# Latents tile by tile from split operands, and other buffers and orders in one hybrid encoder layer

## What is computed

```
h = rmsnorm(x, g_mix);  proj = h @ w_in          # 1024 tokens x 1024
(gq, gk, gv, gr, gaf, gab, cq, ckv, kr, gates) = split(proj)
y_a = gated linear attention of gq, gk, gv, gaf, gab (4 heads, both directions), rmsnorm, silu(gr), @ w_gla_out
q = rmsnorm(cq) @ w_uq;  kv = rmsnorm(ckv) @ w_ukv   # 8 heads, 128 + 64 rotary, values 128
y_b = softmax attention of q, k (rmsnorm per head, rope), v, @ w_mla_out
x = x + (sigmoid(gates_a) * y_a + sigmoid(gates_b) * y_b) @ w_o
h = rmsnorm(x, g_ffn);  16 experts, each takes its top 128 tokens by router softmax
x = x + sum over experts of value * (silu(h @ w_gate) * (h @ w_up)) @ w_down
```

## Time and profile before

| | us |
|---|---|
| runs | 2054.45 median of 3, 2053.08 to 2058.4 |
| profiled execution | 2054.51 |
| its span | 2052.8 |
| TensorE busy | 1939.7 (94%) |
| VectorE busy | 1268.2 (62%) |
| ScalarE busy | 981.9 (48%) |
| mean granted clock of TensorE | 0.981 |
| DMA | 303.11 MB, mean 148 GB/s; 364 GB/s from 1560 on |

### The profile page before, as it was taken

The page is one execution under the profiler, slowest core; times in us unless marked ns, Lnnn a source line. Parts: engine busy times, 40 slices in busy tenths (PEclk is TensorE's granted clock), DMA queues, the critical chain, the costliest instruction groups (busy, mean ns, idle before and its releaser), DMA issues.

```text
span 2052.8 us, 25988 instructions
## 1 busy us (share of the span) xinstructions
PE 1939.7 (94%) x9268; PEld 1605.5 (78%) x9268; DVE 1268.2 (62%) x1660; ACT 981.9 (48%) x1588; POOL 119.4 (6%) x127
## 2 busy tenths in 40 slices
PE   7989999999999999999899999999289999999997
PEld 5677888888778787878688888887278888888886
DVE  4157777777865646565311222432978989898986
ACT  4155555555454334242311211322268787878785
POOL 2010000000000000000000000000001010101010
PEclk9999999999999999999999999999699999999999
DMA  6000000000311111120412311152789999999992
GB/s 238 0 17 12 21 18 22 22 22 6 107 53 43 53 42 52 31 62 9 156 52 65 110 52 52 62 208 90 282 312 380 400 394 399 395 398 397 397 398 80
DMA packets 138658, 303.11 MB, mean 148 GB/s; under 512 B 16208, under 2 KB 70864, under 8 KB 138576
## 3 DMA queue, kind: packets, MB, share of 16 engines
q1 hardware_dynamic: 133968, 285.20, 37.3%
q0 software_dynamic: 4608, 16.78, 3.2%
HBM read 272.58 MB, written 29.36 MB: 147 GB/s over the span
## 4 chain that ended last, share of the span: by engine, by line
PE 87%; DVE 8%; ACT 2%; issue 1%; DMA 1%; POOL 1%; SPq 0%; DVEq 0%; ACTq 0%; POOLq 0%
PE ps L827 21%; PE ps L829 21%; PE ps L828 21%; PE ps L780 6%; PE ps L851 5%; PE ps L808 2%; PE ps L809 2%; PE ps L1042 1%; PE ps L885 1%; PE ps L884 1%; PE ps L1054 1%; DVE row_max L1445 1%; PE ps L1148 1%; PE ps L1026 1%; DVE top_i L1780 1%
## 5 line engine op out<-in xcount | busy, mean ns | idle before, releaser
L1264 DVE TENSOR_TENSOR w_lo<-w_raw,w_hi 128x1024 fp32r<-128x1024 f32 x384 | 442.7, 1218 | 57.8 <-ACT w_hi L2180 57.6
L2180 ACT ACTIVATE w_hi<-w_raw 128x1024 fp32r<-128x1024 f32 x384 | 370.9, 1052 | 12.6 <-PE ps L829 8.0
L1264 DVE TENSOR_TENSOR d_lo<-d_raw,d_hi 128x1024 fp32r<-128x1024 f32 x58 | 71.0, 1224 | 311.9 <-ACT d_hi L1972 311.8
L1972 ACT ACTIVATE d_hi<-d_raw 128x1024 fp32r<-128x1024 f32 x58 | 61.5, 1061 | 308.9 <-PE ps L829 296.9
L827 PE MATMUL ps<-w_hi,xeT_hi 128*128 128x512 f32 x512 | 201.8, 394 | 7.1 <-DVE xeT_lo L1264 7.1
L829 PE MATMUL ps<-w_hi,xeT_lo 128*128 128x512 f32 x512 | 200.1, 391 | 0.0
L828 PE MATMUL ps<-w_lo,xeT_hi 128*128 128x512 f32 x512 | 200.0, 391 | 0.0
L827 PE MATMUL ps<-hT_parts,d_hi 128*128 128x512 f32 x384 | 152.2, 396 | 8.5 <-ACT sg L2105 7.7
L828 PE MATMUL ps<-hT_parts,d_hi 128*128 128x512 f32 x384 | 150.6, 392 | 0.0
L829 PE MATMUL ps<-hT_parts,d_lo 128*128 128x512 f32 x384 | 150.6, 392 | 0.0
L1445 DVE TENSOR_REDUCE row_max<-ps 128x1 f32<-128x1024 f32 x64 | 78.3, 1224 | 106.6 <-PE ps L885 105.9
(11 more groups left out here) (313 smaller groups left out, 4006.7 us busy)
## 6 DMA issues: line engine op xcount, KB each, us to landing
w_raw<-in_w_gate_e SPq DMA_DIRECT2D x128, 512.0 KB, 8.0
w_raw<-in_w_up_e SPq DMA_DIRECT2D x128, 512.0 KB, 7.5
w_raw<-in_w_down_e SPq DMA_DIRECT2D x128, 512.0 KB, 6.7
d_raw<-in_w_in SPq DMA_DIRECT2D x80, 256.0 KB, 3.0
xs<-in_x SPq DMA_DIRECT2D x8, 512.0 KB, 6.9
rows_T<-hT SPq DMA_DIRECT2D x1, 4096.0 KB, 12.8
mla_out_T<-obS SPq DMA_DIRECT2D x16, 256.0 KB, 2.0
carry<-rows_T SPq DMA_DIRECT2D x1, 4096.0 KB, 14.2
```

What stands on the lines that cost most here:

```text
L1264: return dve.tensor_tensor(dst, whole, high.bitcast(F32), ALU.subtract)
L1972: nc.scalar.activation(d_hi[:, n % 2, :], d_raw[:, n % 2, :], ACT.Copy).then_inc(d_hi_ok, 1)
L2180: nc.scalar.activation(w_hi[:, n % RING, :], w_raw[:, n % RAW, :], ACT.Copy).then_inc(hi_ok, 1)
```

## The change

Start and latents. `w_lat` is loaded raw, in four pieces behind x tile 0, and split with the gain inside: ACT `w_lat_hi`, DVE `w_lat_lo`. x is no longer transposed in 16 groups first; `latents(t)` multiplies tile t with `three`, and after its k = 2 transposes tile t + 1 (`x_rows_T`), which ACT splits (`x_high`), DVE completes (`x_low`) and ACT copies to `hT` without the gain (`x_whole`); the gain goes into `rows_high` and `rows_low` at the last head. The transposes of the first half of the latents stand inside tiles 5 to 7 (`LAT_STEP`), with two PSUM banks in turn; those of the second half stand between the first four and the last four projection groups of head 0, which now run 4, 5, 0, 1, 6, 7, 2, 3. `lat_r` lies in `xs`. `hT` is stored in halves, and `load_a2(0)` is issued ahead of it.

GLA heads. The second direction has its own `zT_back`; `gate_bias(1)` does not wait for `ed_ok` and stands ahead of the tail subtraction.

Merge. `sg` lies at 16.5 S, beside `oT_hi` and `oT_lo`; ACT's wait for `oa_out` moves to `branch_hi`.

Experts. In DVE's list of the first turn `rows_in(1)` stands at u = 0 and 2 and `activate(0)` at u = 3; in ACT's list the second part of `rows_in(1)` at u = 6, not 8.

The semaphores `head_ms`, `o_ms`, `x1_ms` and their partners become `mean_sq` and `rstd`, counted through.

```diff
+FIRST_ORDER = (4, 5, 0, 1, 6, 7, 2, 3)
+LAT_STEP = {(5, 4): (0,), (5, 6): (1,), (6, 4): (2,), (6, 6): (3,), (7, 1): (4,), (7, 3): (5,), (7, 5): (6,)}
 @@ memory
-                        w_lat = sb_in(lat_mem, "w_lat", [P, KD, LAT])
-                        lat_r = sb_in(lat_mem, "lat_r", [P, NT, LAT])
+                        lat_r = xs[:, :, 0:LAT]
+                        xT_hi = sb_in(lat_mem, "xT_hi", [P, 2, KD, P], F32R)
+                        xT_lo = sb_in(lat_mem, "xT_lo", [P, 2, KD, P], F32R)
+                    zT_back = sb_in(gla_tmp, "zT_back", [P, S])
-                    sg = sb_in(merge_mem, "sg", [P, 2, S])
+                        sb_in(sg_mem, "below_sg", [P, 16 * S + HALF])
+                        sg = sb_in(sg_mem, "sg", [P, 2, S])
 @@ SyncE
+            load_x(0)
+            sp.dma_start(g_mix_c[:], col(g_mix, KD), allow_slow_non_contiguous=True).then_inc(g_mix_in, 16)
+            for j in range(4):
+                sp.dma_start(w_lat_raw[:, 2 * j:2 * j + 2, :],
+                             w_in_k[:, 2 * j:2 * j + 2, C_LAT:C_LAT + LAT]).then_inc(wlat_in[j], 16)
+            for t in range(1, NT):
+                load_x(t)
 @@ TensorE
+            def x_rows_T(t):
+                pe.wait_ge(xn, t + 1)
+                for b in range(2):
+                    if t:
+                        pe.wait_ge(hT_ok, 2 * t - 1 + b)
+                        pe.wait_ge(xT_lo_ok, 2 * t - 1 + b)
+                    transpose4(b, P, [xs[:, t, (4 * b + j) * P:(4 * b + j + 1) * P] for j in range(4)]).then_inc(hT_tr, 1)
+            def latents_T(c):
+
                 half, j = divmod(c, 7)
                 pe.wait_ge(lat_n, 4 * half + 4)
+                if 2 <= c < 7 or c >= 11:
+                    back = 2 if c < 7 else 4
+                    pe.wait_ge(latT_dve if c % 2 == 0 else latT_act, (c - back) // 2 + 1)
...
+            def latents(t):
+                if t >= 2:
+                    pe.wait_ge(lat_ev, t - 1)
+                a = 4 + 2 * ((t + 1) % 2)
+                hi, lo = xT_hi[:, t % 2], xT_lo[:, t % 2]
+                for k in range(KD):
+                    if k % 4 == 0:
+                        pe.wait_ge(xT_lo_ok, 2 * t + k // 4 + 1)
+                    if t == 0:
+                        pe.wait_ge(wlat_lo_ok, k + 1)
+                    first, last = k == 0, k == KD - 1
+                    three(ps[:, a, 0:LA], hi[:, k, :], lo[:, k, :], w_lat_hi[:, k, 0:LA], w_lat_lo[:, k, 0:LA],
+                          first, last)
+                    mm = three(ps[:, a + 1, 0:LB], hi[:, k, :], lo[:, k, :], w_lat_hi[:, k, LA:LAT],
+                               w_lat_lo[:, k, LA:LAT], first, last)
...
+                    if k == 2 and t + 1 < NT:
+                        x_rows_T(t + 1)
+                    for c in LAT_STEP.get((t, k), ()):
+                        latents_T(c)
...
-            for g in range(4, 8):
+            for g in FIRST_ORDER[0:4]:
                 project(0, g)
-            for g in range(4):
+            for c in range(7, 14):
+                latents_T(c)
+            pe.wait_ge(latT_dve, 7)
+            pe.wait_ge(latT_act, 7)
+            for g in FIRST_ORDER[4:8]:
                 project(0, g)
 @@ VectorE
+            x_mean(0)
             dve.wait_ge(g_mix_in, 16)
+            x_scale(0)
+            for k in range(2):
+                w_lat_low(k)
+            x_low(0, 0)
+            x_low(0, 1)
+            for k in range(2, KD):
+                w_lat_low(k)
+            x_mean(1)
+            x_scale(1)
             dve.wait_ge(small_in, 16 * small_loads)
...
             for t in range(NT):
+                if t + 1 < NT:
+                    x_low(t + 1, 0)
+                    x_low(t + 1, 1)
                 if t:
                     lat_scale(t - 1)
+                if t + 2 < NT:
+                    x_mean(t + 2)
+                    x_scale(t + 2)
+                for c in {6: (0,), 7: (2, 4)}.get(t, ()):
+                    latents_T_in(c)
+                if t == NT - 1:
+                    latents_T_in(6)
+                lat_in(t)
+                lat_mean(t)
...
             def k_mean(h):
-                dve.wait_ge(head_sq, 16 * h + 8)
+                dve.wait_ge(head_sq, 2 * group_count(h, 7))
...
                 def gate_bias(d):
                     dve.wait_ge(z_mm, h * 2 + d + 1)
-                    if d == 1:
-                        dve.wait_ge(ed_ok, h * 2 + 1)
...
                     if d == 1:
                         dense_lo(4, mine)
+                    else:
+                        gate_bias(1)
...
                     if d == 0:
-                        gate_bias(1)
                         dense_lo(3, mine)
...
-                    if first and u in (4, 8):
-                        rows_in(1, (u // 4 - 1,))
+                    if first and u in (0, 2):
+                        rows_in(1, (u // 2,))
+                    if first and u == 3:
+                        activate(0)
 @@ ScalarE
+            act.wait_ge(consts, 4)
+            act.wait_ge(small_in, 16 * small_loads)
+            for t in range(NT):
+                if t + 1 < NT:
+                    for b in range(2):
+                        x_high(t + 1, b)
+                    for b in range(2):
+                        x_whole(t + 1, b)
+                if t + 2 < NT:
+                    x_square(t + 2)
...
+                for c in {6: (1,), 7: (3, 5)}.get(t, ()):
+                    latents_T_in(c)
+                lat_squares(t)
...
-            act.wait_ge(oa_out, 16 * GH)
...
+                        act.wait_ge(oa_out, 16 * GH)
                         act.wait_ge(oa_back, 16 if k < 6 else 32)
```

More of the change, by code:

```diff
@@ L80, with mean_count @@
 EARLY_ROWS = 2
+HEAD_MEANS = 2 * NT
+GLA_MEANS = HEAD_MEANS + 2 * MH
+FFN_MEANS = GLA_MEANS + 2 * GH
+def mean_count(what, t):
+    if what == 0:
+        return t + 1 if t < 2 else 2 * t - 1
+    return 2 * t + 4 if t < NT - 2 else NT + t + 1
 def seam_at(i, n):
@@ L357, in hybrid_layer @@
         small_in = sem("small_in")
-        wlat_in = sem("wlat_in")
+        wlat_in = [sem(f"wlat_in{j}") for j in range(4)]
+        wlat_hi_ok = sem("wlat_hi_ok")
+        wlat_lo_ok = sem("wlat_lo_ok")
         g_mix_in = sem("g_mix_in")
@@ new lines, in w_lat_low, with x_low @@
+            def w_lat_low(k):
+                dve.wait_ge(wlat_hi_ok, k + 1)
+                dve.scalar_tensor_tensor(out=w_lat_lo[:, k, :], in0=w_lat_raw[:, k, :], scalar=g_mix_c[:, k:k + 1],
+                                         in1=w_lat_hi[:, k, :].bitcast(F32), op0=ALU.mult,
+                                         op1=ALU.subtract).then_inc(wlat_lo_ok, 1)
+            def x_low(t, b):
+                dve.wait_ge(xT_hi_ok, 2 * t + b + 1)
+                rows = slice(4 * b, 4 * b + 4)
+                low_part(xT_lo[:, t % 2, rows, :], ps[:, b, :].rearrange("p (a c) -> p a c", a=4),
+                         xT_hi[:, t % 2, rows, :]).then_inc(xT_lo_ok, 1)
@@ L1349, in _ @@
-            for c in range(0, 14, 2):
-                dve.wait_ge(lat_tr, c + 1)
-                dst, src, gain = lat_out(c)
-                dve.tensor_scalar(dst, src, gain, None, ALU.mult).then_inc(latT_dve, 1)
+                if t + 2 < NT:
[6 more added lines that the diff above has]
+                lat_in(t)
@@ L1354, in rotate @@
+                lat_mean(t)
+            lat_scale(NT - 1)
+            for c in range(8, 14, 2):
+                latents_T_in(c)
             def rotate(dst, src, tmp, steps, parts=(0, 1)):
@@ L1977, in out_hi @@
                 nc.scalar.activation(wo_hi[:, u - 2, :], d_raw[:, u % 2, :], ACT.Copy).then_inc(d_hi_ok, 1)
-            for g in range(4, 8):
+            for g in FIRST_ORDER[0:4]:
+                take(0, g)
+            for c in range(7, 14, 2):
+                latents_T_in(c)
+            for g in FIRST_ORDER[4:6]:
                 take(0, g)
             v_high(0)
-            for g in range(4):
+            for g in FIRST_ORDER[6:8]:
                 take(0, g)
+            act.wait_ge(h_out, 32)
+            act.wait_ge(lat_tr, 14)
             for c in (4, 5, 6, 7):
@@ L2207, in turn @@
                 for u in range(UNITS):
-                    if first and u in (4, 8):
-                        rows_in(1, (u // 4 - 1,))
+                    if first and u in (4, 6):
+                        rows_in(1, (u // 2 - 2,))
                     split(FIRST + u, e)
```

274 lines of the change are left out of this document (141 added, 133 removed).

## The result

The changed kernel takes **2026.21 us** (median of 4 runs, 2024.85 to 2030.54), the kernel before 2054.33 in the same series (2053.08 to 2058.40). The ratio is **0.9863, 95% interval 0.9843 to 0.9883**. The forecast was 2028.7 in a range of 2015 to 2044. The profiled execution has a span of 2024.5 us for 2052.8, 28.3 less.

A forecast was written before the change was run, and what follows sets the result against it. TensorE, busy 94% of the span, was taken as the bound: its work plus waits. Start -6.9, GLA heads -8.5, merge -3.3 and experts -7.1 sum to -25.8, from 2054.5 to 2028.7 us; range 2015 to 2044.

The forecast's parts named there:

- Start: Latents to first scores: first scores at 136.7 us against 143.6, so -6.9, bounds -11 to +10.
- this cover: Start: small loads landing at 24.2, then DVE's angles of 6.2 us, hold tile 1's latents until 31.1.
- The k step: Latents: six narrow products, 2208 columns, take 1.00 us; far bound 1.36.
- Rival 1: Latents: narrow products no quicker than 512-column ones, step 1.36, total 2045.5 us; chance 0.08.
- the waits 0.93 and 3.13: Tiles 6 and 7: TensorE waits 0.9 and 3.3 us for DVE's copies ahead of `latents_T(2)` and `latents_T(4)`.
- rivals 3 and 4: Start: 3, waits in every tile keep the clock low, 2076, chance 0.05; 4, gain lost in waits, 2047 to 2059, 0.07.
- the slow stretch behind the wait at tile 7: Latents: 1.6 us added for TensorE running slow after its 3.3 us wait at tile 7.
- GLA: GLA heads: four waits for `zT`, 6.9 us, go, with a slow stretch of 1.6: -8.5, bounds -5 and -9.5.
- Merge: Merge's start: ACT, freed from `oaS`'s store, waits for a weight landing at 984.2: -3.3, bounds -1 and -8.
- Experts: First expert's turn: `rows_in(1)` ahead of `activate(0)` and first splits moves TensorE's transposes earlier: -7.1, bounds -5 and -8.
- The other edits: Gain in `rows_high` and `rows_low`, shared semaphores, earlier `load_a2(0)`, halved h store: worth nothing, under 1 us without cover.
- Rival 2: Waits of the start or merge absent, or a stretch at full clock: 10 to 14 us more, 2015 to 2018; chance 0.10.

The follow-up runs named there:

- the eight: Eight profiles whose start is the changed kernel's code: its own two and six kernels with later parts undone or altered; first scores 136.5 to 142.1 us, median 139.3.
- Experiments 1 and 2: Changed kernel with one shared `zT` in the old order: 2039.5 us; with `zT_back` kept but `gate_bias(1)` back behind `decay`: 2034.2 us (one run).
- second profile: The changed kernel, nothing altered, profiled and run once more: 2030.9 us, first scores at 140.8 us.
- the median of nine: Nine profiles that have the changed kernel's code at the merge's start; that part runs from 42.3 to 43.8 us, median 43.2.
- Experiment 4: Changed kernel with the merge's third weight unit issued ahead of the 3 MB read of `mT`, not behind it: 2021.3 us, ratio 0.9831.
- 9 to 11: Changed kernel with angles behind tile 0: 2023.7 us; DVE's copies first: 2024.0; start reordered: 2016.9, and with the merge's unit ahead of the read: 2010.4.
- the last two kernels: Changed kernel with the start reordered: 2016.9 us; the same with the merge's third weight unit ahead of the 3 MB read: 2010.4 us.

## Why the prediction held, point by point

**Start, -6.9 forecast; -7.1 in the first profile, some -4 over the eight.** Step by step: small loads issued last at 20.85 and landed at 24.7 (24.2 forecast), angles 6.2 us, tile 1 at 31.55 (31.1). DVE's timeline, which answers to the earlier trace rows, shows this cover exactly:

```profile
24.71 0.15 DVE L1390 TENSOR_SCALAR qhn_c<-qhn_c 128x1 f32<-128x1 f32 x1 [5.35 <-DMA w_router_s<-in_w_router]
...
30.60 0.29 DVE L1414 TENSOR_SCALAR cos_t<-cos_t 128x256 f32<-128x256 f32 x1
30.81 1.28 DVE L1314 TENSOR_TENSOR xT_lo<-ps,xT_hi 128x512 fp32r<-128x512 f32 x2
```

The k step is 1.01 (42.22 to 43.23; 1.00 forecast): a 416-column product starts every 0.190 us, a 320-column one every 0.147, which is 17 and 14 ns over their columns at 2.4 GHz, as the 14 ns of 512 columns. Rival 1 (narrow products no quicker) is out. The Trainium skill (TensorE: Matmul & The Clock Gate, Back-to-back issue gap) gives columns over clock plus 2.5 ns for a product by itself; an estimate by it is 0.94 for the step, and the trace does not agree. For a stream of weight loads and products the same section has about 131 ns for 512 columns; the 227 ns of the earlier trace rows do not agree with that either. A tile took 8.93 (8.9), the waits 0.93 and 3.13 (0.9 and 3.3), the wait for `k_norm` 2.01 (2.2), the latents ended at 102.4 (102.8), no tile in the middle waited, and the clock was 1.00 from 41 to 84 in all eight profiles: rivals 3 and 4 are out. What the forecast treats as one number differs from execution to execution. For the slow stretch behind the wait at tile 7 I put 1.6 us; it is 0 in two executions and 1.3 to 2.8 in six, 1.5 in the mean. Two things are missing from the sum: the second slow stretch, 1.7 us in four of the eight, and tile 7's restart, forecast at 93.8, came at 94.9 to 96.2, as tile 1 stayed at the lower clock for different lengths. The first profile had neither slow stretch, which made up for a tile 1 that ended 0.8 late: that it hit -6.9 so closely is luck. The kernel before varies too: its runs lie between 2052.0 and 2059.1, but there is one profile of it, without a fall before its first scores.

**GLA, -8.5 forecast, -10.5 measured.** The mechanism was right in each part: the waits go, no new one comes, the buffer carries most. The term that was mis-sized is the price of a wait. The forecast took the idle time, 6.9, and one slow stretch, 1.6. Experiments 1 and 2 add 0.3 us for each wait, 1.2 in all, and a wait of 0.25 for `carry` in the last head went with them; the last 0.5 I can't place. Against the two profiles with `zT` shared the part is worth 11.4, as the clock there fell behind two of the waits and not one.

**Merge, -3.3 forecast, -3.8 measured** (-2.2 by the second profile, -2.8 by the median of nine). The wait's own share came to 2.3 for 3.3: the unit was split 12.6 us after its issue, not 11.6, so TensorE waited 5.35, not 4.5. The slow stretch behind it, which I let stay whole, gave 1.4 more in the first profile (0.50 for 3.4 us) and nothing in the second. Two errors of about 1 us that offset each other. Experiment 4 shows that the landing was the bound.

**Experts, -7.1 forecast, -6.9 measured,** with waits of 0.27 and 0.61 for 0.1 and 0.9; the transposes start 31.2 us after expert 0's first product, 38.1 before. The other edits, put at nothing, are worth nothing that the parts can show: the rest of the span agrees within 0.1 us.

**Rivals.** Rival 2 (waits of the start or merge not there) did not come: the waits are there to 0.2 and 0.9 us, though the stretch at full clock, one of its conditions, did in the first profile. Experiments 4 and 9 to 11 show what that rival would have been worth.

What stays open: what decides whether the clock falls behind a given idle. After 3.13 us of it, it fell in six executions of eight; after one of 2.0 for `kRr`, in four of the same eight; after one of about 2 us in the heads, once in three in the kernel before and in two of three in both kernels with `zT` shared, in different heads.

## What to carry to other kernels

When a stage is cut into tiles, look at what each queue carries ahead of the second tile: here one block of DVE work that nobody needed yet cost 5 to 9 us of the start, and the cut with its splits, without the cheaper products, was a loss. In this kernel a wait in a full TensorE stream cost its idle plus about 0.3 us, and in part of the executions 1.3 to 2.8 us more; count the waits, not only their sum. And compare a small part by landmarks within the profile, since the 5.6 us by which the start varied hide it in the total.

## What was not expected of the hardware

The same program runs at a different granted clock behind the same wait from one execution to the next: behind the 3.13 us idle at tile 7 the mean over 10 us was 1.00 in one profile and 0.71 in the other (1.00 is 2.4 GHz, half of it the lower level), 2.6 us of time. In the ten runs of the new start alone, all on one chip, the mean granted clock goes with the time without an exception, from 0.979 at 2045.7 us to 0.975 at 2054.1. Where a wait was removed, as at the merge in experiment 4, the clock stayed at 1.00, and the last two kernels, with the fewest waits, scatter by 3 us over five runs each, where the new start alone scattered by 8.4 over ten; so few runs only hint that the one comes of the other.
